# Layer 1's sparse attention: compressed logits with the queries moving in column tiles, logits and a rotation moved up, the result turned and projected by token tiles

## What is computed

```python
# layer 1, nsa_attention; u (256, 1024), 16 heads of 64, 4 key/value groups, 4 blocks of 64 tokens
proj = u @ w_in
q = rmsnorm(proj[..., :hd].reshape(B, S, N_HEADS_B, HEAD_DIM), q_gain)
gates = jax.nn.sigmoid(proj[..., hd:] + b_gate).reshape(B, S, N_HEADS_B, 3)
q_rot = apply_rope(q, cos, sin)
logits = einsum('bsghd,bngd->bsghn', q_plain, k_cmp) * HEAD_DIM ** -0.5     # compressed branch
p_cmp = where(vis, softmax(where(vis, logits, -1e30)), 0.0)
o_cmp = einsum('bsghn,bngd->bsghd', p_cmp, v_cmp)
# with 4 blocks all are selected, so the other two branches are causal softmax attention of q_rot
# over k_sel, v_sel and k_win, v_win
o = gates[..., 0:1] * o_cmp + gates[..., 1:2] * o_sel + gates[..., 2:3] * o_win
return o.reshape(B, S, hd) @ w_o
```

## Time and profile before

| | us |
|---|---|
| median of 3 runs | 1452.88 |
| lowest, highest | 1445.59, 1455.73 |
| the profiled execution | 1451.8 |
| its span on the core | 1450.0 |
| TensorE busy in the span | 1396.2 |
| DVE, ACT busy | 321.2, 266.2 |

### The profile page before, as it was taken

The page is one execution under the profiler, slowest core; times in us unless marked ns, Lnnn a source line. Parts: engine busy times, 40 slices in busy tenths (PEclk is TensorE's granted clock), DMA queues, the critical chain, the costliest instruction groups (busy, mean ns, idle before and its releaser), DMA issues.

```text
span 1450.0 us, 20506 instructions
## 1 busy us (share of the span) xinstructions
PE 1396.2 (96%) x8353; PEld 801.7 (55%) x8353; DVE 321.2 (22%) x776; ACT 266.2 (18%) x518; POOL 31.1 (2%) x77
## 2 busy tenths in 40 slices
PE   5999899999999999999989998989999999999997
PEld 1677766545544444444368777864564444444442
DVE  1330523111111111111132567241111111111111
ACT  2211523110111111111023355131100111111110
POOL 5000000000100000000000000000010000000000
PEclk9999999999999999999999968999999999999999
DMA  9999289899999999999998500138999999999997
GB/s 378 410 420 419 103 327 405 356 387 421 364 420 421 421 420 421 421 421 421 421 417 318 217 1 1 59 119 363 421 387 398 421 420 421 421 421 421 421 421 287
DMA packets 71599, 512.30 MB, mean 353 GB/s; under 512 B 8240, under 2 KB 8432, under 8 KB 9552
## 3 DMA queue, kind: packets, MB, share of 16 engines
q1 hardware_dynamic: 70560, 509.64, 85.4%
q0 software_dynamic: 800, 1.25, 0.4%
q10 hardware_dynamic: 144, 0.08, 0.0%
HBM read 509.89 MB, written 1.05 MB: 352 GB/s over the span
## 4 chain that ended last, share of the span: by engine, by line
PE 89%; DMA 5%; DVE 3%; ACT 2%; issue 1%; SPq 0%; DVEq 0%; ACTq 0%; POOLq 0%
PE PS L918 23%; PE PS L533 13%; PE PS L908 12%; PE PS L926 12%; PE PS L942 11%; DMA ring<-in_w_exp 3%; PE PS L560 3%; PE PS L675 2%; PE PS L954 2%; DMA ring<-in_w_ada_units 1%; PE PS L514 1%; PE PS L658 1%; PE PS L544 1%; PE PS L963 1%; PE PS L934 1%
## 5 line engine op out<-in xcount | busy, mean ns | idle before, releaser
L918 PE MATMUL PS<-ring,scratch 128*32 128x512 f32 (+2 forms) x2176 | 355.4, 597 | 6.6 <-DMA ring<-in_w_exp 5.3
L918 PEld LDWEIGHTS PS<-ring,scratch 128*32 128x32 f32 (+2 forms) x2176 | 111.5, 123 | 243.2 <-issue 241.5
L908 PEld LDWEIGHTS PS<-scratch,u 128*128 128x128 f32 x1600 | 183.0, 192 | 38.6 <-issue 36.8
L908 PE MATMUL PS<-scratch,u 128*128 128x128 f32 x1600 | 192.5, 278 | 1.4 <-ACT scratch L1142 1.4
L926 PE MATMUL PS<-ring,scratch 128*32 128x512 f32 (+2 forms) x1088 | 182.2, 596 | 2.3 <-DVE item_first_i L1258 1.2
L942 PE MATMUL PS<-scratch 128*128 128x512 f32 x384 | 172.7, 592 | 0.0
L1278 DVE TENSOR_TENSOR scratch<-PS,gate_row 128x512 f32<-128x512 f32 x100 | 69.2, 692 | 461.5 <-PE PS L926 461.5
L533 PE MATMUL PS<-ring,uT 128*128 128x256 f32 x768 | 170.9, 381 | 0.0
L533 PEld LDWEIGHTS PS<-ring,uT 128*128 128x128 f32 x768 | 144.7, 191 | 25.4 <-issue 6.5
L1150 ACT ACTIVATE scratch<-PS 128x256 f32<-128x256 f32 x50 | 19.2, 384 | 674.5 <-PE PS L918 674.5
L926 PEld LDWEIGHTS PS<-ring,scratch 128*32 128x32 f32 (+2 forms) x1088 | 52.6, 122 | 122.3 <-issue 120.6
(11 more groups left out here) (324 smaller groups left out, 832.8 us busy)
## 6 DMA issues: line engine op xcount, KB each, us to landing
ring<-in_w_exp SPq DMA_DIRECT2D x384, 1024.0 KB, 16.5
ring<-in_w_ada_units SPq DMA_DIRECT2D x56, 1024.0 KB, 15.4
ring<-in_w_in_a_units SPq DMA_DIRECT2D x12, 1024.0 KB, 23.4
ring<-in_w_cmp_units SPq DMA_DIRECT2D x8, 1024.0 KB, 26.3
ring<-in_w_sh_units SPq DMA_DIRECT2D x6, 1024.0 KB, 13.6
ring<-in_w_kv_b_units SPq DMA_DIRECT2D x6, 1024.0 KB, 22.4
ring<-in_w_o_a_units SPq DMA_DIRECT2D x4, 1024.0 KB, 9.3
ring<-in_w_in_b_units SPq DMA_DIRECT2D x4, 1024.0 KB, 10.7
```

The costliest lines, as they stand in the source:

```text
L908: mm = pe_.matmul(PS[:, bank, i * w:(i + 1) * w], u[:, t, k * P:(k + 1) * P], hot[:, t, :], start=(t == 0), stop=(t == NT - 1))
L918: mm = pe_.matmul(PS[places, GU, :], x[:, kk, places], gate_and_up, start=(kk == 0), stop=(kk == KC - 1))
```

## The change

Four edits of order and one of form:

- `w_forget` is loaded by the first instruction of POOL's queue. POOL also makes `own_group`, a 0/1 matrix that picks a head pair's own group.
- Compressed logits: `kcz` whole (32 columns: 2 heads by 4 groups by 4 blocks) is the weight and 256 query columns move, for the four column tiles of the array in turn; 8 matmuls give the products of every query with all groups' keys. ACT copies them (512 columns) to `cmp_raw`, which lies over `ada_parts`, and 4 matmuls with `own_group` pick the right group's and turn them back, ahead of the first turning of probabilities.
- `turn_plain(2)` moves into `queries(3)`, whose bank is now 3; the turning of rotated tile 2 moves up to the gates' product, and logits 0 and 1 go between the last turnings. DVE rotates tile 2 ahead of the norm of tile 3. DVE copies the gates after the first two masks.
- The turned result has a bank per token tile and half of the width: 16 matmuls of 128 columns for the compressed heads, and token tile 0 is turned, copied and projected (`out_b(0, 0)`) before token tile 1 is turned.

```diff
+            pool.dma_start(w_forget[:, :, :], a["w_forget"]).then_inc(forget_loaded, 16)
             done(pool.memset(eps_col[:, :], EPS))
...
+            done(pool.memset(own_group[:, :], 0.0))
+            done(pool.affine_select(out=own_group[:, :], in_=own_group[:, :], compare_op=ALU.not_equal, fill=1.0, base=0,
+                                    pattern=[[-36, G], [-16, 2], [-1, NB]], channel_multiplier=1))
...
-            pool.dma_start(w_forget[:, :, :], a["w_forget"]).then_inc(forget_loaded, 16)
...
-        Q_BANK = [1, 2, 0, 1]
+        Q_BANK = [1, 2, 0, 3]
...
-            pe_.wait_ge(sem("q_normed"), 1)
-            queries(3)
+            queries(3, lambda: turn_plain(2))
             turn_rotated(1)
-            turn_plain(2)
             pe_.wait_ge(sem("kcz_ready"), 2)
             pe_narrow(pe_, w_gates, 6, u_queries, 3 * H, sem("gates_out"))
+            turn_rotated(2)
...
+            pe_logits(pe_, "nsa", nsa_batches, nsa_keys, 0)
             turn_plain(3)
-            turn_rotated(2)
+            pe_logits(pe_, "nsa", nsa_batches, nsa_keys, 1)
+            pe_.wait_ge(sem("gates_active"), 1)
+            pe_narrow_rows(pe_, narrow_T[0:3 * H, :], narrow_rows(6, SEQ, 3 * H)).then_inc(sem("gates_turned"), 1)
             turn_rotated(3)
...
-            for t in range(NT):
-                for pair in range(H // 2):
-                    g = pair // 2
-                    mm = pe_.matmul(cmp_logits[:, t, 2 * pair:2 * pair + 2, :], uT[:, pair, t * P:(t + 1) * P],
-                                    kcz[:, :, g * NB:(g + 1) * NB], start=True, stop=True)
-            mm.then_inc(sem("cmp_logits"), 1)
+            for q in range(2):
+                for i in range(G):
+                    mm = pe_.matmul(PS[32 * i:32 * i + 32, 7, q * SEQ:(q + 1) * SEQ],
+                                    kcz[:, :, :].rearrange("p a b -> p (a b)"), uT[:, 2 * i + q, :],
+                                    start=True, stop=True)
+            mm.then_inc(sem("cmp_raw"), 1)
+            def pick_cmp_logits(b):
+                if b == 0:
+                    pe_.wait_ge(sem("cmp_raw_copied"), 1)
+                    pe_.wait_ge(sem("gates_ready"), 1)
+                    for t in range(NT):
+                        for q in range(2):
+                            at = q * SEQ + t * P
+                            mm = pe_.matmul(cmp_logits[:, t].rearrange("p (g q a) n -> p q g (a n)", g=G, q=2)[:, q],
+                                            cmp_raw[:, at:at + P],
+                                            own_group[:, :].rearrange("p (g c) -> p g c", g=G), start=True, stop=True)
+                    mm.then_inc(sem("cmp_logits"), 1)
...
-            def turned(k):
-                return PS[:, k // 2, (k % 2) * SEQ:(k % 2 + 1) * SEQ]
+            def turned(t, k):
+                return PS[:, 2 * t + k // 4, (k % 4) * P:(k % 4 + 1) * P]
...
+                for t in range(NT):
+                    for k in (0, 4, 1, 5, 2, 6, 3, 7):
+                        rows = slice(32 * (k // 4), 32 * (k // 4) + 32)
+                        pe_.matmul(turned(t, k),
+                                   v_diag[rows, 2 * (k % 4):2 * (k % 4) + 2, :].rearrange("p h d -> p (h d)"),
+                                   cmp_T[rows, t * P:(t + 1) * P], start=(k % 4 == 0), stop=False, skip_group_check=True)
...
+            out_b(0, 0)
             for g in range(4):
                 pe_.wait_ge(sem("nsa_o"), 4 + g + 1)
                 add_turned(1, 2 * g)
-                add_turned(1, 2 * g + 1).then_inc(rows_turned, 1)
...
+                add_turned(1, 2 * g + 1)
+            out_b(1, 0)
+            out_b(0, 1)
+            out_b(1, 1)
+            pe_gate(pe_, 2)
+            for t in range(NT):
+                out_b(2, t)
+            pe_last_quarter(pe_, AT["out_b", 3], 1)
...
             act_table(act, ACT.Exp)
+            act.wait_ge(sem("cmp_raw"), 1)
+            done(act.activation(cmp_raw[:, :], PS[:, 7, :], ACT.Copy), sem("cmp_raw_copied"))
...
-            act_copy_turned(done, uT, "nsa_o")
+            for bank in range(4):
+                t, c = bank // 2, bank % 2
+                act.wait_ge(rows_turned, 4 * TURNED.index("nsa_o") + bank + 1)
+                if bank == 1:
+                    act.wait_ge(heads_out, 8 + len(nsa_batches))
+                done(act.activation(uT[:, 4 * c:4 * c + 4, t * P:(t + 1) * P],
+                                    PS[:, bank, :].rearrange("p (k t) -> p k t", k=4), ACT.Copy), rows_copied)
...
+            rotate(2)
             query_norm(3)
-            rotate(2)
             rotate(3)
-            dve.wait_ge(sem("gates_turned"), 1)
-            done(dve.tensor_copy(gates[:, :, :], narrow_rows(7, 0, 3 * H)), sem("gates_ready"))
...
                 if b == 0:
+                    dve.wait_ge(sem("gates_turned"), 1)
+                    done(dve.tensor_copy(gates[:, :, :], narrow_rows(6, SEQ, 3 * H)), sem("gates_ready"))
                     cmp_scores()
```

## The result

| us | before | after |
|---|---|---|
| median | 1450.13 (13 runs) | 1440.51 (13 runs) |
| lowest, highest | 1445.11, 1459.25 | 1435.77, 1450.69 |
| the profiled execution | 1451.8 | 1438.07 |
| its span | 1450.0 | 1436.3 |

The ratio is 0.9936 with a 95% interval of 0.9914 to 0.9958: the change is worth 9 us, within 1% of before, as forecast (1441.6 for the median). The lowest runs differ by 9.3 us and the highest by 8.6. The two profiled executions differ by 13.7 us, 4 more than the medians. To see where they come from I cut both spans at four instructions: the start of layer 1's last query tile (Q), the third and the sixteenth attention mask of the nsa attention (M3, M16) and the start of the last unit of the output projection (L).

What follows compares the result with a forecast made beforehand. TensorE, busy 96% of the span, was taken as the bound, with everything behind it a rigid train. From 1451.8: -2.9 -8.8 +0.6 -0.2 = 1440.5, plus 1.1 for the median: 1441.6 us, range 1433 to 1449.

Steps and rivals of the forecast that it cites:

- The forget weights: At the front, loading them first in POOL's queue lets TensorE's forget product start sooner: 2.9 us saved, between 1.0 and 4.7.
- The opening: Start of layer 1's nsa attention: third mask 7.3 us sooner, then 1.5 more to the sixth mask, 8.8 in all.
- Of it, 6 come from 32 instructions at half clock becoming 24 short ones: Opening, compressed logits: 6 of the 7.3 us gained to the third mask were credited to the new form.
- only one gap of over a microsecond: Opening: TensorE would idle over a microsecond only once, 838.5 to 839.7, so full clock was assumed there.
- 1.5 more: Third to sixth mask: at full clock DVE is the bound, 9.2 to 9.3 us are left of 10.7, saving 1.5.
- From there the batches are alike: Nsa attention behind the sixth mask: batches take the same time as before, no further gain or loss.
- Part 2: Start of layer 1's attention, new order and logits form: 8.8 us saved, 6.4 at half clock as low end.
- The "slower" rival: Nsa attention: 24 us of half clock move onto narrow and wide batches, costing 16.5 us; 1458, chance 0.05.
- the clock rivals: Half clock at the nsa opening, 1444, chance 0.19; full clock at the tail too, 1436, chance 0.21.
- So +0.6 taken: Tail, compressed heads: 32 instructions of 128 columns cost 0.6 us more than 16 of 256; range -0.3 to +3.7.
- the -0.2 for the earlier projection: Tail: the output projection's first half-unit begins right behind the last weighing, saving 0.2 us.
- The rival of full clock at the tail: Tail, 894 to 911: shifted work meets the clock better, saving 5.8 us more; 1436, chance 0.21.

Runs made afterwards that it cites:

- the old logits: The changed kernel with the old form of the compressed logits (16 matmuls, no copy or pick) in the new order: median 1446.08 us, ratio 0.9962 to the kernel before.
- second profile: The changed kernel run again unaltered, beside two variants, and profiled once more: median 1437.19 us (12 runs), ratio 0.9933 to the kernel before.
- the weights behind: The changed kernel with DVE's compressed-weight operations moved behind the sixth mask: medians 1437.33 us and, repeated, 1437.56 us; ratios 0.9903 and 0.9913 to the kernel before.
- the old tail: The changed kernel with the old layout and order behind attention, 8 compressed-head products of 256 columns: median 1443.57 us, ratio 0.9964 to the kernel before.
- the kernel with three moves: The changed kernel with compressed weights behind the sixth mask, Exp table load before the last rotated copy, gates' copy before the first mask: median 1438.18 us, ratio 0.9914.
- the kernel with the filled gap: The changed kernel with seven unread products added ahead of the weighing of batch 4: median 1441.70 us, ratio 0.9928 to the kernel before.
- the kernel with moves and fill: The changed kernel with three reordered DVE and ACT steps, plus three unread products before weighing batches 4, 12 and 13: medians 1434.95 and, repeated, 1433.52 us.

## Why the prediction was right, and where only the sum was

**The forget weights: right.** 2.7 us in the profile after and 2.8 in the kernel that has this edit alone, 2.9 forecast from the middle of 1.0 and 4.7. The middle was a lucky pick in a range that is real: the twelve profiles with the edit show 1.7 to 4.4, by the clock in the product, and the change's second one 1.8. The operand was ready at 30.7 instead of 30.35, and the product took 5.30, between full and half clock as assumed. That the saving passes the slots' wait unchanged was the reading of the earlier trace rows, and held.

**The opening: the first half right, its reason partly wrong, the second half wrong.** To the third mask the schedule gave 7.3 and it was 7.3. The step "Of it, 6 come from 32 instructions at half clock becoming 24 short ones" credits the new form. But the old product with the new order takes 3.80 and reaches the third mask sooner. In the old order TensorE stands 0.78 and 1.17 us ahead of the product and the clock falls at about its start, in the kernel before and in the one with the old order and the new logits; in the new order it stands once, for 1.03 us, and the product is over or nearly over when the clock falls (836.6 with the old logits, 839.7 after, not at all in the opening of the second profile). So the clock was about half of what I charged to the form: 3.2 of the 6.99 us. The schedule's "only one gap of over a microsecond" was two, 1.03 and 1.32 us. The step "1.5 more" to the sixth mask came as 0.9 in the first profile and 1.35 in the second, where the clock didn't dip at 840 (M3 to M6 of 9.8 and 9.4, before 10.7). The step that failed is **"From there the batches are alike"**. They are alike only at the same speed of TensorE: the compressed weights, ahead of the sixth mask, had stood beside a TensorE at half clock, and uncovered they cost a stall, with a fall of the clock behind it, and 2.5 us from the sixth to the sixteenth mask (38.5 against 36.0). Part 2 is worth 5.7 (6.0 in the second profile), not 8.8. The "slower" rival named this mechanism, half clock on wide batches, in a much larger size; one batch was hit, by way of a stall that I had not looked for. It was in reach: with the third mask 7.3 sooner, each instruction of DVE in the next ten microseconds had to be asked what it keeps TensorE waiting for.

The Trainium skill (TensorE: Matmul & The Clock Gate, Part 4) kept the clock rivals alive in the prediction by its remark on transposes. The runs show the fox attention, which is as full of them, at 1.00 in both profiles of the change and eight others and at 0.50 in three (the weights behind, twice, and the old tail), so neither the row of 1.00 in the earlier trace rows nor the rule alone could decide it.

**The tail: term mis-sized.** "So +0.6 taken": I priced the 32 instructions at 0.09 each from 64-row weights. They cost 0.064, 2.05 us in all, and the 16 wide ones, which I had put at 2.2 at full clock, 2.00: +0.05. With the -0.2 for the earlier projection the tail was to cost 0.4; it gains 0.3.

**The rival of full clock at the tail** (0.21) is what both profiles of the change show: 36.6 us from M16 to L against 43.4 before, 6.7 us where I had put 5.8. It is not an effect of the edit there, for the same tail took 45.7 in two of its variants. Nor is it rare: nine of the eleven profiles with the changed order or a variant of it have the full clock there, and of the change's 25 runs 17 lie from 1435.8 to 1441.7 and 8 from 1445 to 1450.7. Both profiles with the old opening had the fall (43.4, and 41.1 with the forget weights alone), so that the change as a whole may make it rarer; that stays open. My view of one clock history with small terms around it was too simple; a run of this kernel falls or doesn't fall at some places, for 1 us (behind the wide batch in the kernel with three moves) to 9 us (the tail) each. I can't say from these runs what decides it.

**The sum.** Of the 13.7 us between the profiles 3.2 lie before Q, 5.7 to M16, 6.7 in the tail, and 1.9 are lost behind it. Without the tail's clock, and without the router's behind it, the forecast terms give 3.2 + 5.7 + 0.3 = 9.2 (2.1 + 6.0 + 0.3 = 8.4 by the second profile), and the medians differ by 9.6. The forecast saving was 11.3: the front came out 0.3 better, the opening 3.1 worse, the tail 0.7 better, and 0.4 is unaccounted for. That the 1441.6 was yet only 1.1 us off owes something to the median before, which was 2.8 lower than the one I had started from (1450.1, not 1452.9) and hid the 1.7 that the saving fell short: that the sum came so close is luck in part.

## What to carry to other kernels

When work that ran at half clock becomes fast, whatever other engines had put beside it loses its cover: follow the new, earlier times one pipeline length further and look at what stands ahead of each mask or copy in an in-order queue. A packed form of small products pays against the old form at the old clock; try the reordering alone first, since the product may then meet the full clock and leave the form little to win. When single profiles differ by more than the medians, cut both spans at the same instructions and take out the stretches whose clock differs before pricing an edit.

## What the runs showed of the hardware

- 32 instructions with 32-row weights and 128 columns each took 2.05 us, 16 with 256 columns 2.00; at half clock both took 3.8 (3.78 for the wide ones, 3.79 for the narrow ones in the kernel with the old logits). The count of instructions didn't matter at this size, the columns did.
- 16 instructions in four column tiles, with 256 columns each, took 1.07 us. L1614's price per instruction from the earlier trace rows (0.9 for 16) was a fair guide.
- A product of few columns with 128 columns of weights still follows the clock: the same 32 instructions took 6.99 us nearly all at 0.50, and 3.80 with all but the last half microsecond at 1.00.
- The clock stood at 0.50 with TensorE busy: 14.7 of 15 us busy at a mean of 0.56, from 836 to 851 in the kernel with the filled gap.
- The length of a stall alone doesn't decide whether the clock falls. Stalls of 2.56 to 2.57 us had a fall behind them in three profiles of three. But ahead of batch 5's weighing 1.65 us had one (three moves) and 1.66 and 1.67 had none (weights behind, twice), and 1.17 us had one in the first profile of the kernel with moves and fill and none in the second. At the tail a stall of 1.43 us stood ahead of a fall in the kernel before and of none in both profiles of the change.
